# Hybrid attention block on one core: who splits one gate weight, and where the first steps of attention A stand

## The reference

```python
h = rms_norm(x, g_mix)
z = h @ w_in                       # q, k, v of A | c_q, c_kv, k_rope of B | gate_A, gate_B
y_a = swa_sink_attention(qa, ka, va, positions, ...)   # window of 128, ALiBi, sinks, 8 heads of 64, 2 kv heads
y_b = mla_attention(cq, ckv, krope, positions, ...)    # low-rank q and kv, rotary, chunk-causal, 8 heads
gt = sigmoid(gates + b_gate)       # 2 x 1024 columns
merged = gt[A] * (y_a @ w_branch_a) + gt[B] * (y_b @ w_branch_b)
x = x + merged @ w_out
x = x + relu(rms_norm(x, g_mlp) @ w_ff1)^2 @ w_ff2
```

## Time and profile before

| | |
|---|---|
| three runs | 1405.85, 1409.25, 1409.51 us |
| median | 1409.25 us |
| the profiled execution | 1409.92 us, of which the span from the first to the last instruction is 1407.8 us |
| mean granted clock of PE | 0.999 of 2.4 GHz |
| busy share of the span | PE 97%, PE weight loads 80%, DVE 58%, POOL 53%, ACT 29% |

### The profile page before, as it was taken

The page is one execution under the profiler, slowest core; times in us unless marked ns, Lnnn a source line. Parts: engine busy times, 40 slices in busy tenths (PEclk is TensorE's granted clock), DMA queues, the critical chain, the costliest instruction groups (busy, mean ns, idle before and its releaser), DMA issues.

```text
span 1407.8 us, 17512 instructions
## 1 busy us (share of the span) xinstructions
PE 1369.6 (97%) x6612; PEld 1122.2 (80%) x6612; DVE 819.1 (58%) x1420; ACT 407.1 (29%) x856; POOL 747.4 (53%) x599
## 2 busy tenths in 40 slices
PE   6999998999999999999998999999999999999998
PEld 6999786778866766888887888888888888888876
DVE  5401814542577773455265567776666767766695
ACT  5113134652355654000033212221221222122120
POOL 2331923345385520354307566667766666776691
PEclk9999999999999999999999999999999999999999
DMA  7120221111120112735101112211121212111112
GB/s 230 45 61 25 81 90 60 55 55 45 42 57 13 13 16 58 241 102 193 40 24 49 48 45 60 61 43 48 53 59 39 60 60 58 41 53 53 40 43 120
DMA packets 102739, 90.81 MB, mean 65 GB/s; under 512 B 21888, under 2 KB 84864, under 8 KB 102656
## 3 DMA queue, kind: packets, MB, share of 16 engines
q1 hardware_dynamic: 102512, 89.17, 21.1%
q10 hardware_dynamic: 144, 0.52, 0.1%
HBM read 76.99 MB, written 12.62 MB: 64 GB/s over the span
## 4 chain that ended last, share of the span: by engine, by line
PE 88%; DVE 5%; POOL 3%; ACT 2%; issue 2%; DMA 1%; DVEq 0%; SPq 0%; ACTq 0%; POOLq 0%
PE PS L1420 74%; PE PS L1614 3%; PE PS L1427 2%; PE PS L1513 1%; PE PS L1564 1%; PE PS L1535 1%; PE PS L1594 1%; PE PS L1515 1%; PE PS L1784 1%; PE PS L1595 1%; PE PS L1596 1%; PE PS L1578 1%; PE PS L1550 1%; POOL b_rstd L867 1%; ACT gate L1184 1%
## 5 line engine op out<-in xcount | busy, mean ns | idle before, releaser
L2183 DVE TENSOR_TENSOR xr<-PS,xr 128x512 f32<-128x512 f32 x240 | 161.8, 685 | 83.6 <-PE PS L1420 83.6
L1420 PE MATMUL PS<-w_hi,u_hi 128*128 128x512 f32 x420 | 163.7, 390 | 5.5 <-issue 3.5
L2183 DVE TENSOR_TENSOR sum<-PS,sum 128x512 f32<-128x512 f32 x168 | 113.8, 686 | 87.2 <-PE PS L1420 87.2
L1420 PE MATMUL PS<-w_hi,u_lo 128*128 128x512 f32 x420 | 163.6, 390 | 0.0
L1420 PE MATMUL PS<-w_lo,u_hi 128*128 128x512 f32 x420 | 163.6, 390 | 0.0
L1420 PE MATMUL PS<-mT_hi,w_hi 128*128 128x512 f32 x512 | 160.9, 390 | 0.0
L1420 PE MATMUL PS<-mT_lo,w_hi 128*128 128x512 f32 x512 | 160.6, 390 | 0.0
L1420 PE MATMUL PS<-mT_hi,w_lo 128*128 128x512 f32 x512 | 160.5, 390 | 0.0
L1043 POOL TENSOR_TENSOR w_lo<-w_raw,w_hi 128x512 fp32r<-128x512 f32 x109 | 155.6, 1428 | 9.1
L1355 ACT ACTIVATE relu_t<-PS 128x512 f32<-128x512 f32 x64 | 38.3, 598 | 301.0 <-PE PS L1420 298.1
L858 POOL TENSOR_SCALAR w_hi<-w_raw 128x1024 fp32r<-128x1024 f32 x32 | 38.7, 1209 | 160.1 <-DMA w_raw<-in_w_ff 160.1
(11 more groups left out here) (234 smaller groups left out, 2954.7 us busy)
## 6 DMA issues: line engine op xcount, KB each, us to landing
w_raw<-in_w_ff SPq DMA_DIRECT2D x32, 512.0 KB, 4.1
w_raw<-in_w_ff SPq DMA_DIRECT2D x64, 256.0 KB, 2.6
g_raw<-in_w_in SPq DMA_DIRECT2D x16, 512.0 KB, 3.9
gate_store<-gate SPq DMA_DIRECT2D x16, 512.0 KB, 2.6
x_in<-in_x SPq DMA_DIRECT2D x8, 512.0 KB, 10.4
gate_a<-gate_store SPq DMA_DIRECT2D x8, 512.0 KB, 7.6
gate_b<-gate_store SPq DMA_DIRECT2D x8, 512.0 KB, 5.1
raw<-in_w_out SPq DMA_DIRECT2D x8, 512.0 KB, 3.5
```

The costliest lines, as they stand in the source:

```text
L1420: ins = pe.matmul(o, st, cut(mv), start=first and n == 0, stop=last and n == 2)
L2183: dve.tensor_tensor(out, part, out, ALU.add).then_inc(acc_done, 1)
```

## The change

Four edits. (1) The high half of gate 4's weight is written by ACT, behind `gate_out(2)`; POOL writes only the low half, behind three waits. (2) On ACT `gate_out(3)` moves ahead of the pads, the distances and `v_even`, and PE's first small transpose no longer waits for it. (3) Attention A begins at point 27 in place of 28: step 0 at point 27, step 1 at 28, none at 29, and from step 2 at point 30 on as before, on all four engines. (4) At points 28, 32, 36 and 40, the first of a gate, PE does `scores(k)` (k = 1, 4, 8, 12) ahead of the gate's products and their wait.

```diff
--- before.py
+++ after.py
@@ -67,7 +67,7 @@
 BW_RING = 4
 POINTS = 4
 SMALL_AT = 18
-A_AT = 28
+A_AT = 27
 PROJ_AT = 47
 TURNS = {55: (8, 9), 56: (10, 11), 58: (12, 13), 59: (14, 15)}
 SHIFTS = {57: (0, 1), 58: (2, 3), 60: (4, 5), 61: (6, 7), 62: (8, 9), 63: (10, 11)}
@@ -523,7 +523,8 @@
 
         def a_step(p):
 
-            return p - A_AT if 0 <= p - A_AT < N_A + 3 else None
+            k = p - A_AT if p < A_AT + 2 else p - A_AT - 1
+            return k if p != A_AT + 2 and 0 <= k < N_A + 3 else None
 
         def first_group(p):
 
@@ -910,7 +911,10 @@
             z_power(2)
             gate_split(3)
             z_power(3)
-            gate_split(4)
+            pool.wait_ge(graw_landed[0], 48)
+            pool.wait_ge(gate_done, 3)
+            pool.wait_ge(gw_hi_done, 5)
+            pool.tensor_tensor(gw_lo[0][:, :, :], g_raw[0][:, :, :], gw_hi[0][:, :, :], ALU.subtract).then_inc(gw_ready, 1)
             gate_split(5)
             pool.memset(kaT[:, :, 0:CHUNK], 0.0).then_inc(ka_pad_ready, 1)
             pool.memset(pos_row[:, 0:CHUNK], 0.0).then_inc(ka_pad_ready, 1)
@@ -1213,11 +1217,14 @@
             z_square(6)
             z_square(7)
             gate_out(2)
+            act.wait_ge(graw_landed[0], 48)
+            act.wait_ge(gw_hi_done, 4)
+            act.activation(gw_hi[0][:, :, :], g_raw[0][:, :, :], ACT.Copy).then_inc(gw_hi_done, 1)
+            gate_out(3)
             act.wait_ge(ka_pad_ready, 2)
             dist_half()
             act.activation(v_even[0:CHUNK, 1:T, :], Zv[CHUNK:P, 0:T - 1, :], ACT.Copy).then_inc(v_even_ready, 1)
             act.activation(v_even[CHUNK:P, :, :], Zv[0:CHUNK, :, :], ACT.Copy).then_inc(v_even_ready, 1)
-            gate_out(3)
 
 
             def group_act(g, p):
@@ -1473,7 +1480,6 @@
             def small_transpose(n):
                 if n == 0:
                     pe.wait_ge(z_normed, 5 * T)
-                    pe.wait_ge(gate_ready, 4)
                 if n >= 4:
                     wait_small_read(pe, n - 4)
                 h = n // 6 if n < 12 else (n - 12) // 3
@@ -1629,14 +1635,17 @@
                     ins.then_inc(gate_done, 1)
 
             for p in range(2 * KD * POINTS):
+                k = a_step(p)
+                early = k is not None and k < N_A and p % POINTS == 0
+                if early:
+                    scores(k)
                 gate_chunks(p // POINTS, p % POINTS)
                 for n in small_at(p):
                     small_transpose(n)
-                k = a_step(p)
                 if k is not None:
                     if 2 <= k < N_A + 2:
                         p_transposes(k - 2, 0)
-                    if k < N_A:
+                    if k < N_A and not early:
                         scores(k)
                     if k >= 3:
                         values(k - 3)
```

## The result

| | before | after |
|---|---|---|
| median | 1408.76 us (6 runs, 1405.85 to 1409.51) | 1402.06 us (6 runs, 1398.85 to 1402.58) |
| profiled execution | 1409.92 us, span 1407.8 | 1399.27 us, span 1397.4 |

The ratio is 0.9947, with a 95% interval of 0.9937 to 0.9956: 6.7 us, or 0.53%, faster. The forecast was 1403.2 us and a gain of 6.05.

The account below looks back on a forecast made before the run. PE, busy 97% of the span, was taken as the bound, with 7.1 us of waits to close. Gains 1.00 + 1.65 + 3.1 + 0.3 = 6.05 us gave 1403.2 us from a median of 1409.25; range 1400.2 to 1406.5.

Parts of the forecast that it names:

- Wait 1: PE's wait for gate 4's low-half weights from POOL: gate 4 starts at 171.45 instead of 172.45, gain 1.00 us.
- rival A: POOL gets its turn early on gate 4 and that wait closes whole: gain 7.0, 1402.2 us; chance 0.15.
- Wait 2: PE's wait at the first small transpose for gate 3's sigmoid goes away: gain 1.65 us, nearly certain.
- Wait 3: PE's sigmoid stall at gate 7, filled by scores(0) and scores(1), up to the first `scA` transposes: gain 3.1 us.
- rival B: Gate 4's wait stays whole and the first transposes' spare microsecond is used up: gain 3.6, 1405.6 us; chance 0.2.
- The wait of step 1: PE's second wait for POOL's scaling of `scA`, 0.93 us at 233.33, was forecast to stay.
- Early scores at 32, 36 and 40: Scores ahead of the gate's products at three later points in attention A: between -0.3 and +0.6, gain 0.3 us.
- Rival C: The wait for gate 3's sigmoid hid another equally late one; only the scores count, 1405.9 us; chance 0.04.
- Rival D: Slower: new pauses in attention make the clock fall repeatedly, six stretches costing 10.2 us, 1413.4 us; chance 0.04.
- The sign of being wrong: First transposes still waiting for POOL, or a pause of the same size ahead of the B heads, would refute the forecast.

Follow-up runs that it names:

- e9: The kernel after with its first edit undone, POOL writing both halves of gate 4: 1402.54 us, ratio 0.9964 to the kernel before.
- e6: The kernel after plus one DVE wait for its own instructions, ahead of every second tile of z's normalization: 1401.11 us, ratio 0.9948 to the kernel before.
- e10: The kernel after, unchanged, run again for a second profile: 1400.79 us, ratio 0.9952 to the kernel before.
- e2: The kernel before with the second edit alone, gate 3's sigmoid first and no wait at the first small transpose: 1407.91 us, ratio 0.9997.
- e7: The kernel after with DVE's reciprocal of step 1 at empty point 29 instead of point 30: 1400.67 us, ratio 0.9947 to the kernel before.
- e4: The kernel after with early scores at point 28 only, not at 32, 36 and 40: 1401.31 us, ratio 0.9955 to the kernel before.

## Why the prediction was right, point by point

**Wait 1**, gate 4: forecast 1.00, measured 1.13 (172.45 - 126.84 = 45.61, now 170.90 - 126.42 = 44.48), in e9 1.14. POOL got in at the place named, behind DVE's line 1912. The Trainium skill's rule of an exclusive lock, from "SBUF — State Buffer", section "Who interferes with whom", read as one instruction at a time, would have given 1.96, and with it rival A. Measured: a split shown for 9.22 us, of which 2.35 is its own length, was held over some twenty DVE instructions (five for each tile of positions, not seven as the kernel's description above has it). So for these operations the turn did not change between instructions that follow each other without a stop, nor at a wait already met; e6 shows that it does where DVE has to stop. The measurement decides against the strict reading. That whichever starts first holds the other is borne out, by the rows near 500 us under e10. And the engines do not "meet only through semaphores", as the description above says: DVE and POOL also hold each other.

**Wait 2**: forecast 1.65, measured 2.77 - 1.13 = 1.64, where 2.77 us is what the first small transpose gained against gate 0 (55.55 us behind it before, 52.78 after); alone in e2, 1.71.

**Wait 3 and the first transposes**: T is 211.36 + 0.45 = 211.81, the transposes are at 221.83, T + 10.0 as forecast, against 13.12 before; gain 3.1. DVE's copy of the sinks did fall on POOL's split of gate 8 and took 1.75 us. POOL in the kernel after, which answers to the earlier trace rows:

```profile
218.98 1.47 POOL L980 TENSOR_TENSOR scA<-scA,a_rsum 128x768 f32<-128x768 f32 x1 [3.31 <-DVE a_rsum L2023]
```

It ends at T + 8.6; the forecast was T + 8.9. The spare time was real, and rival B, which needed it used up, did not occur. The wait of step 1 stayed, 0.89 for 0.93, and e7 shows the reason given for it, DVE's order.

**Early scores at 32, 36 and 40** is the term that was mis-sized: forecast 0.3, measured 6.76 - 2.77 - 3.10 = 0.89, and 0.88 by e4. I had counted only waits that the list names, 0.45 us, and set a cost of 0.1 us for each lone scores against them. The gaps ahead of the transposes are larger than their brackets and one of three has none: by the distances under e4 they are 0.78 us. The cost that I feared does not show: the three places gained 0.30, 0.31 and 0.26 us against gaps of 0.19, 0.27 and 0.32. Whether a lone scores costs anything was not measured by itself.

Rival C is excluded by e2. Rival D did not occur: the windows of attention stayed at full clock, and the one fall was there or not there by the execution. The range had room for it, rightly: single runs of the kernel after span 3.7 us. (Its lower end, 1402.2 - 1.7, is 1400.5; the prediction rounds it to 1400.2. Nothing hangs on that, with 1402.06 measured.) The sign of being wrong, a pause of the same size ahead of attention B, did not appear: the two profiles are 7.18 us apart at gate 12 and 7.22 at 500 us.

The time itself was missed by 1.1 us. Of this 0.65 is the gain (6.70 by the medians against 6.05), and 0.5 is that six runs of the kernel before have a median of 1408.76 and the first three one of 1409.25. By M, where the scatter is small, the sum fell short by 0.7 us, of which 0.6 is the one term, the three later places, and 0.13 is wait 1.

## What to carry to other kernels

When two waits of the critical engine stand in series, the first is worth its size only if the second goes with it; price them as a pair. Work that is due anyway is best placed ahead of a wait for another engine, not behind it, even where that wait is a few tenths: at a boundary that recurs, gaps too short for the list of waits add up, so measure the distance between starts. An engine that is held by a long unbroken series of another may be let in by one cheap wait inside the series, but it must be one at which the other has to stop. Where effects are near the scatter of whole runs, measure a distance between two landmarks of the trace around the change.

## What the runs showed of the hardware

Before the runs I did not expect that a single semaphore wait in DVE's list would decide whether POOL's instruction is shown for 9.22 us or 2.87, and that a wait already met would not. Nor that one program, with the same pause of 3.5 us on PE, would drop to 1.2 GHz in one execution and not in another, at 1.55 us; that, 0.70 us for a transfer of attention B and 0.35 the other way ahead of gate 0 make the 1.9 us by which two profiles of the same kernel differ in span, where M differs by 0.01. And a transfer that lands about 0.1 us earlier or later can decide which of DVE and POOL is held, at 1.1 us of PE.
